# A retention stage with 64-column states, transposes moved between the matmuls of the projections, and own-block scores in front of the state products

## The reference

```python
def chunk_retention(q, k, v, lg, s0, inclusive):        # chunks of 128 tokens
    scores = jnp.einsum('bhnid,bhnjd->bhnij', qc, kc) * dmat[None, :, None]
    o_inner = jnp.einsum('bhnij,bhnje->bhnie', scores, vc)
    wk = jnp.exp((c - 1 - i)[None, :] * lg[:, None])
    u = jnp.einsum('bhnjd,hj,bhnje->bhnde', kc, wk, vc)  # 64 x 64 for each head and chunk
    def step(s, u_n):
        return g_chunk * s + u_n, s
    _, s_prev = lax.scan(step, s0, jnp.moveaxis(u, 2, 0))
    wq = jnp.exp((i + 1)[None, :] * lg[:, None])
    o_cross = jnp.einsum('bhnid,hi,bhnde->bhnie', qc, wq, s_prev)
    return (o_inner + o_cross).reshape(b, h, l, dv)
```

## Time and profile before

| | us |
|---|---|
| median of 3 runs (lowest, highest) | 3538.36 (3535.79, 3541.39) |
| the profiled execution | 3541.91 |
| its span | 3540.1 |
| PE busy in the span | 3165.1 (89%) |
| DVE, ACT, POOL busy | 1487.3, 790.2, 1078.6 |
| mean granted TensorE clock | 0.948 |

### The profile page before, as it was taken

One profiled execution on the slowest core, in us unless ns is written; L12 is line 12 of the kernel. 1 busy time (PEld: TensorE's weight loads), 2 busy tenths in 40 slices (PEclk: granted clock), 3 DMA queues, 4 the chain that ended last, 5 costly groups with the idle time before them and its releaser, 6 DMA issues.

```text
span 3540.1 us, 39903 instructions
## 1 busy us (share of the span) xinstructions
PE 3165.1 (89%) x16718; PEld 2552.8 (72%) x16718; DVE 1487.3 (42%) x1661; ACT 790.2 (22%) x983; POOL 1078.6 (30%) x497
## 2 busy tenths in 40 slices
PE   6986998999789599898888999999699999999959
PEld 5866886787478478787556678787478888888737
DVE  2135508514522631743576630323654044144375
ACT  1110215311220111421134420112222111011241
POOL 1222220023122223023323334343134444444323
PEclk8988999999899799999889999999899999999979
DMA  5200011322021001112121111112111111111111
GB/s 222 72 24 1 30 45 40 109 102 91 22 105 36 7 23 44 49 43 101 36 77 36 36 42 48 38 49 95 71 42 47 48 48 47 48 52 48 60 59 71
DMA packets 57216, 200.64 MB, mean 57 GB/s; under 512 B 5632, under 2 KB 7424, under 8 KB 57088
## 3 DMA queue, kind: packets, MB, share of 16 engines
q1 hardware_dynamic: 40224, 135.81, 11.4%
q10 hardware_dynamic: 16864, 62.97, 4.7%
HBM read 180.93 MB, written 17.83 MB: 56 GB/s over the span
## 4 chain that ended last, share of the span: by engine, by line
issue 40%; PE 34%; POOL 14%; DVE 8%; DMA 2%; ACT 1%; POOLq 0%; ACTq 0%; SPq 0%; DVEq 0%
PE ps L512 26%; POOL w_hi L445 8%; POOL w_lo L447 6%; DVE Sb L1471 3%; PE ps L742 2%; DVE ST L1413 2%; DMA raw<-s 1%; PE ps L659 1%; DMA modfirst<-modw 1%; PE ps L539 1%; PE ps L591 1%; DVE h_lo L1292 1%; DVE kw L1383 1%; PE ps L829 1%; PE ps L763 1%
## 5 line engine op out<-in xcount | busy, mean ns | idle before, releaser
L445 POOL TENSOR_TENSOR w_hi<-raw,pool_zero 128x1024 fp32r<-128x1024 f32 (+1 forms) x228 | 423.5, 1858 | 2260.6 <-PE ps L512 2238.7
L447 POOL TENSOR_TENSOR w_lo<-raw,w_hi 128x1024 fp32r<-128x1024 f32 (+1 forms) x228 | 619.8, 2718 | 17.9
L512 PE MATMUL ps<-g_hi,w_hi 128*128 128x512 f32 x1600 | 503.5, 396 | 37.8 <-DVE g_lo L1292 36.1
L512 PE MATMUL ps<-h_hi,w_hi 128*128 128x512 f32 (+1 forms) x1856 | 474.6, 362 | 56.8 <-DVE h_lo L1292 48.8
L512 PE MATMUL ps<-g_lo,w_hi 128*128 128x512 f32 x1600 | 495.9, 391 | 0.0
L512 PE MATMUL ps<-g_hi,w_lo 128*128 128x512 f32 x1600 | 495.3, 391 | 0.0
L512 PE MATMUL ps<-h_lo,w_hi 128*128 128x512 f32 (+1 forms) x1856 | 455.6, 352 | 0.0
L512 PE MATMUL ps<-h_hi,w_lo 128*128 128x512 f32 (+1 forms) x1856 | 455.2, 352 | 0.0
L512 PEld LDWEIGHTS ps<-h_hi,w_hi 128*128 128x128 f32 x1856 | 305.0, 190 | 128.4 <-issue 63.6
L512 PEld LDWEIGHTS ps<-g_hi,w_hi 128*128 128x128 f32 x1600 | 302.2, 190 | 111.8 <-issue 39.1
L512 PEld LDWEIGHTS ps<-g_lo,w_hi 128*128 128x128 f32 x1600 | 302.8, 189 | 63.6
(11 more groups left out here) (276 smaller groups left out, 3359.8 us busy)
## 6 DMA issues: line engine op xcount, KB each, us to landing
raw<-s SPq DMA_DIRECT2D x212, 512.0 KB, 3.2
modring<-modw ACTq DMA_DIRECT2D x32, 512.0 KB, 4.9
xin<-xT ACTq DMA_DIRECT2D x1, 5120.0 KB, 15.1
x_saved<-Y ACTq DMA_DIRECT2D x1, 5120.0 KB, 17.0
xin<-x_saved ACTq DMA_DIRECT2D x1, 5120.0 KB, 17.8
modfirst<-modw SPq DMA_DIRECT2D x4, 1024.0 KB, 10.9
modfirst<-modw ACTq DMA_DIRECT2D x4, 1024.0 KB, 19.3
x_saved<-Y ACTq DMA_DIRECT2D x1, 4096.0 KB, 11.7
```

What stands on the lines that cost most here:

```text
L445: G.tensor_tensor(w_hi[s][:, :n], raw[s][:, :n], zero.to_broadcast([P, n]), ALU.add).then_inc(hi_done, 1)
L447: G.tensor_tensor(w_lo[s][:, :n], raw[s][:, :n], w_hi[s][:, :n].bitcast(F32), ALU.subtract)\
L512: last = T.matmul(ps[:, o + c0:o + c0 + size], wt[s][:, kk], xx[:, k, t0:t0 + size], start=(k == 0 and n == 0), stop=(k == k_n - 1 and n = ...
```

## The change

Five things, in both layers.
1. **States of 64 columns.** `ST` is 128 x 64 per state: head 0 on partitions 0 to 63, head 1 on 64 to 127. A state product becomes two matmuls of 64 x 64, one per head. A step of the chain becomes one instruction on 128 partitions for both heads, and the two directions alternate, so it waits for the products of both. An output takes one matmul per head and direction with 64 rows and 64 columns of weights, in place of one per direction. The clearing of `ST` goes.
2. **Work moved between the matmuls of slabs.** The rotations move from behind slab g0+6+c to behind k = 7, 6, 5, 4, 3, 2 of it. The values are transposed in three groups of ten tiles inside slabs g0+9 (k = 2 and 5) and g0+11 (k = 2) into banks 0 to 2, and the keys of pair 0 inside slab g0+11 (k = 6). The values of the neighbourhood branch are transposed inside slab g0+18 (k = 2, 4, 6) into banks 3 to 5.
3. **Tables earlier.** DVE's table work stands ahead of the ropes, ACT's behind slab g0+7. Memory is laid out anew for that (`Dm`, `WQ`, `dtmp` in the place of `kw`, `kw` in that of the cosines and sines).
4. **Banks and waits.** Scores and later keys use banks 4 and 5, outputs banks 6 and 7, products banks 0 to 3. The wait for ACT's last copy moves from ahead of slab g0+12 to the first norm matmul in it. POOL's second group of queries no longer waits for the products.
5. **Key weighting** is one tensor_tensor per direction over both heads in place of two tensor_scalar.

```diff
-        ST = at("ST", W_YNA, [P, 2, NT, P])
+        ST = at("ST", W_YNA, [P, 2, NT, HD])
...
-                        if i == 1:
-                            pool.wait_ge(u_ready, 2 * (3 * l + p) + 2)
-                        elif q + i:
+                        if i != 1 and q + i:
                             pool.wait_ge(o_ready, q + (1 if i else 0))
...
+                for c in range(6):
+                    def beside(k):
+                        if l == 0 and c == 0 and k == 4:
+                            turn_modulation(1, [7 * BANK, 7 * BANK + P])
+                        if k == (7, 6, 5, 4, 3, 2)[c]:
+                            if l == 0 and c == 0:
+                                pe.wait_ge(mod_added, 1)
+                            rotate(c)
+                        if c == 3 and k in (2, 5):
+                            if k == 2:
+                                pe.wait_ge(evac_done, g0 + 9)
+                            turn_values(6 * l + k // 3, 0)
+                        if c == 5 and k == 2:
+                            pe.wait_ge(evac_done, g0 + 11)
+                            turn_values(6 * l + 2, 0)
+                        if c == 5 and k == 6:
+                            pe.wait_ge(vt_used, 6 * l + 3)
+                            for gi in range(3):
+                                turn_pair_keys(0, gi)
+                    if c == 4:
+                        pe.wait_ge(vt_used, 6 * l + 2)
+                    slab(g0 + 6 + c, c % 2, h_hi, h_lo, KD, (FULL, part)[c % 2], 3, between=beside)
+                pe.wait_ge(evac_done, g0 + 12)
...
                         for x, d in enumerate(terms):
-                            T.matmul(ps[:, c:c + P], ST[:, d, STATE_AT[d](n), :], qw[i % 2][:, d, t * P:(t + 1) * P],
-                                     start=(t == 0 and x == 0), stop=False, skip_group_check=True)
+                            for a in range(2):
+                                r = slice(HD * a, HD * (a + 1))
+                                T.matmul(ps[r, c:c + P], ST[r, d, STATE_AT[d](n), :], qw[i % 2][r, d, t * P:(t + 1) * P],
+                                         start=(t == 0 and x == 0), stop=False, skip_group_check=True)
...
                         for x, n in enumerate(BACK if d else range(NT - 1)):
-                            b = 3 * d * BANK + x * P
-                            last = T.matmul(ps[:, b:b + P], kw[:, d, n, :], Vt[:, n, p * P:(p + 1) * P],
-                                            start=True, stop=True)
+                            for a in range(2):
+                                c = 2 * d * BANK + x * HD
+                                last = T.matmul(ps[HD * a:HD * (a + 1), c:c + HD], kw[:, d, n, HD * a:HD * (a + 1)],
+                                                Vt[:, n, p * P + HD * a:p * P + HD * (a + 1)], start=True, stop=True,
+                                                skip_group_check=True)
                         last.then_inc(u_ready, 1)
...
-                pe.wait_ge(o_used, o_groups(l, PAIRS))
...
+                slab(g0 + G_NA + 6, 0, h_hi, h_lo, KD, part, 3, between=values)
+                pe.wait_ge(vt_used, 6 * l + 6)
...
+                    dve.wait_ge(u_ready, 2 * (3 * l + p) + 2)
+                    for x in range(NT - 1):
+                        for d in range(2):
+                            c = 2 * d * BANK + x * HD
+                            if x == 0:
+                                ins = V.tensor_copy(ST[:, d, 0, :], ps[:, c:c + HD])
+                            else:
+                                ins = V.scalar_tensor_tensor(ST[:, d, x, :], ST[:, d, x - 1, :], gch[:, 3 * d + p:3 * d + p + 1],
+                                                             ps[:, c:c + HD], ALU.mult, ALU.add)
```

More of the change, by code:

```diff
@@ L576, in _ @@
                         slab(j * 2 + (g0 + s), s, h_hi, h_lo, KD, (FULL, part)[s], 3, between=gates if l == 0 else None)
[L577 to L592, removed]
-                                            start=True, stop=True)
-                        last.then_inc(rot_ready, 1)
@@ L596, in _ @@
[L596 to L610, removed]
@@ L612, in _, with turn_values @@
-                transpose_values(18 * l)
-                pe.wait_ge(vt_used, 18 * l + 9)
-                ku = 9 * l
+                def turn_values(unit, base):
+                    if unit % 3:
+                        pe.wait_ge(vt_used, unit)
+                    for n in range(NT):
+                        last = T.transpose(ps[:, base * BANK + n * P:base * BANK + (n + 1) * P],
+                                           VT[:, unit % 3, n * P:(n + 1) * P], ident)
+                    last.then_inc(vt_ready, 1)
@@ L616, in turn_pair_keys, with rotate @@
+                def rotate(c):
+                    pe.wait_ge(tab_in, 48 * (l + 1))
+                    pe.wait_ge(rope_done, 6 * l + c + 1)
+                    for half in range(2):
+                        last = T.matmul(ps[:, (6 + half) * BANK:(7 + half) * BANK], ret_const[:, 0, :],
+                                        QK[:, c, CTX + 512 * half:CTX + 512 * (half + 1)], start=True, stop=True)
+                    last.then_inc(rot_ready, 1)
                 def turn_pair_keys(p, gi):
@@ L618, in turn_pair_keys @@
                     n0, cnt = GROUPS[gi]
[L619 to L624, removed]
+                    u = 9 * l + 3 * p + gi
+                    if p == 0:
+                        bank = gi
+                    else:
+                        bank = 4 + (3 * p + gi) % 2
+                        if 3 * p + gi >= 5:
+                            pe.wait_ge(kt_used, u - 1)
+                        if gi == 0:
+                            pe.wait_ge(sd_ready, o_groups(l, p))
@@ L714, in _, with values @@
                         slab(j * 2 + (g0 + G_NA + s), s, h_hi, h_lo, KD, FULL, 3, between=norms)
-                slab(g0 + G_NA + 6, 0, h_hi, h_lo, KD, part, 3)
-                pe.wait_ge(evac_done, g0 + G_NA + 6)
-                transpose_values(18 * l + 9)
+                def values(k):
+                    if k == 2:
+                        pe.wait_ge(evac_done, g0 + G_NA + 6)
+                    if k in (2, 4, 6):
+                        turn_values(6 * l + 3 + (k - 2) // 2, 3)
+                slab(g0 + G_NA + 6, 0, h_hi, h_lo, KD, part, 3, between=values)
+                pe.wait_ge(vt_used, 6 * l + 6)
                 slab(g0 + G_NA + 7, 1, h_hi, h_lo, KD, part, 3)
@@ L1006, in _ @@
-                evac_values(18 * l)
+                    if c == 1:
+                        evac_values(6 * l, 0)
+                        evac_values(6 * l + 1, 0)
+                    if c == 2:
+                        evac_values(6 * l + 2, 0)
+                    evac_part(g0 + 7 + 2 * c, Y[:, 2 + c, :], ACT.Silu)
+                    if c == 0:
+                        act.wait_ge(dtab, l + 1)
+                        lgl = lg[:, 18 * l:18 * l + 18]
+                        A.activation(Dm[:], dtmp[:], ACT.Exp)
+                        for d in range(2):
+                            for p in range(PAIRS):
+                                x = 12 + 3 * d + p
+                                A.activation(WQ[:, d, p, :], ret_const[:, 3 + d, :], ACT.Exp, scale=lgl[:, x:x + 1])
+                        own.link(A.activation(wk[:], wk[:], ACT.Exp))
+                        A.activation(gch[:], lgl[:, 12:18], ACT.Exp, scale=float(P)).then_inc(wtab, 1)
@@ L1038, in _ @@
                     taken(1, VT)
+                for c in range(3):
+                    evac_values(6 * l + 3 + c, 3)
                 act.wait_ge(bias_clear, 2 * l + 1)
```

129 lines of the change are left out of this document (54 added, 75 removed).

## The result

| | before | changed |
|---|---|---|
| median, us (lowest to highest, runs) | 3539.3 (3535.79 to 3541.39, 4) | 3449.28 (3448.16 to 3450.42, 4) |
| profiled execution | 3541.91 | 3448.83 |
| span | 3540.1 | 3445.9 |
| PE busy in the span | 3165.1 (89%) | 3131.7 (91%) |
| mean granted TensorE clock | 0.948 | 0.957 |

The ratio is 0.9747, with a 95% interval of 0.973 to 0.9764: 90 us faster, where 61 were forecast.

A forecast was written before the change was run, and what follows sets the result against it. The retention stage was taken as bound by a chain across engines for which PE waits. Savings of 30.2 us in layer 0 and 30.8 in layer 1, together 61.0, took the median 3538.36 to 3477, given as 3478; range 3463 to 3500.

The forecast's parts named there:

- the copy of slab 11: Behind slab 11 PE first waits for ACT's copy of it: 1.5 us in layer 0, 1.3 in layer 1.
- the weighting: Key weighting of the first pair: four tensor_tensor of 512 columns and two of half the size, 3.4 us in all.
- POOL hidden: POOL's weight split and queries behind slab 11 finish before they are needed, with 6 us spare.
- slab 12 right behind the last outputs: At the stage's end PE no longer waits for ACT's last copy: 1.1 us saved in each layer.
- Products 4.36 to the chain's start: In each retention pair, the chain starts 4.36 us after the products, since it waits for both directions.
- no change, nearest to the 64-column row: The 72 recorded loads of narrow products take 3.9 us, the same as the 4.09 before.
- the lower bound of 2.0 us: Products of a pair if only the moving columns counted, now half: 2.0 us, 2.1 less.
- rival 2: Products at half their time and a warm clock during the chain's wait: 3458 to 3470, chance 0.16.
- That is one half, 5.53: The chain of states, nine steps of two instructions for both directions together, takes 5.53 us per pair.
- 0.197 each: Price of a transpose moved into a slab; 40 of them make 7.9 us, in slabs lengthened by 10.2 per layer.
- The values of the neighbourhood branch: Their 30 transposes, moved into the slab, cost 6.0 + 0.3 us: 0.4 and 0.7 lost, perhaps 0.1 for the last copy.
- Rivals 1, 3 and 4: Narrow tiles no faster, 3502 or 3525, chance 0.12; clock falls inside slabs, 3614, 0.02; moved work meets waits in slabs, 3498, 0.06.

The follow-up runs named there:

- e2: Changed kernel with all nine state products of one head ahead of those of the other, within each direction: 3454.1 us.
- e4: Changed kernel with each chain instruction on 128 partitions split by head into two on 64, direction outer, head inner: 3489.1 us.
- e3: Changed kernel with the products of both directions of a step in neighbouring columns of one PSUM bank: 3449.01 us.
- e6: Changed kernel with each chain instruction split by head into two on 64 partitions, head outer, direction inner: 3474.06 us.
- e5: Changed kernel with all chain steps of one direction, then the other, the first starting when its own products are done: 3448.62 us.
- e1: Changed kernel with each value transpose issued twice in a row, 120 more in all, inside slabs: 3464.22 us.
- v6: Changed kernel with the matmuls of the second scores issued four times, in the time in which PE idles: 3432.93 us.
- v9: Changed kernel with v8's order and waits, and the second scores issued twice in layer 0 and three times in layer 1: 3428.03 us.
- v1: Changed kernel with products issued step by step, both directions together, and the chain starting behind the first four steps: 3437.32 us.
- v8: Changed kernel with products step by step as in v1, the chain starting once its first step's products are done: 3432.08 us.
- e7: Changed kernel with rotations back behind their slabs and the first pair's values and keys transposed behind slab 11, narrow states kept: 3485.33 us.

## Why the prediction was wrong

What was right: the stage as a row of waits, the copy of slab 11 as the first wait (1.3 to 1.5), the weighting (3.15 for six against 3.4), POOL hidden, slab 12 right behind the last outputs, the clock full in the slabs, and the direction. The steps that failed are three prices in the sum, all off in one direction.

1. **"Products 4.36 to the chain's start."** It was 2.36 (239.75 to 242.11), 2.0 less in each of six pairs, 12 us. I took "no change, nearest to the 64-column row" and left the lower bound of 2.0 us as rival 2. The price holds for two products of the same head: e2 shows 0.052 per record where I gave 0.054. That it is the loads that set this pace was argued, and no run tests it. But products of two heads write different halves of the partitions and run together. The Trainium skill, TensorE: Matmul & The Clock Gate, "What overlaps and what doesn't", has it that a weight load overlaps a running matmul only in other row groups. The trace disagrees: the 72 loads, all on the same 128 rows, take 2.18 us, and their matmuls 2.32 in the same stretch (rows at 239.74 and 259.29; the end of a matmul is modelled in the profile).
2. **"That is one half, 5.53."** It was 4.42, 1.1 less per pair, 6.6 us. Halving the instructions was right. What the halving left out is that the old chain's neighbours changed the half of the partitions at every instruction and so started 0.302 and 0.322 apart (e4), while two directions on the same partitions start 0.20 apart (e3 on 128, e6 on 64). My bounds for it, "the same" and 0.7 more, left nothing below the half. In e5 the forecast's 5.53 comes out, as 5.43, because there each instruction waits for the last.
3. **"0.197 each" for transposes.** That mean had the waits for ACT in it: PE was idle in 1.6 of the 5.90 us for 30. In a slab nothing waits, and e1 gives 0.11 to 0.12. The slabs got 6.1 longer in each layer and not 10.2: 4.1 x 2 = 8.2. The values of the neighbourhood branch won 2.6 and 2.3 where 0.4 and 0.8 were to be lost: 6.1.

Together 12 + 6.6 + 8.2 + 6.1 = 32.9; with the 61 of the forecast 94, and the spans differ by 94.2. That it closes so well is in part luck: the profiled execution before lay 2.6 above its median, the medians differ by 90, and parts that the change does not touch move by some us between profiles.

Rival 2 was nearest, by its first half. Its second half, a clock that stays full since PE idles less, did not come: the clock still fell in every pair, and only in the second of layer 0 after the first outputs. v6 and v9 show that this was there to be had, 1.8 us a pair in v6. There PE idled 0.75 to 1.65 us before the first outputs and the clock never fell in the two stages; in v1, with 2.27 and 2.49, it fell in none of three pairs and in all three; in v8, with 1.94 and 2.17, in two and in all three; in the changed kernel, with 3.4 to 3.7, in all six. What else decides beside the idle time is open. Rivals 1, 3 and 4 fell: no row of the slabs runs below the full clock or waits.

## What to carry to other kernels

Look for the rate of an instruction in its distance to the next start, not in its length, and ask for each neighbour whether it uses the same partitions and whether it depends on the one before. A price for work that is to be moved is to be taken from a row without waits. Where PE waits for a chain on another engine, count what it costs twice: the wait, and the slower matmuls behind it; either can be worked on by itself, as v6 did with the second and v8 with the first. Whether the clock falls is to be read from the trace, not from the length of the wait alone.

## What the runs showed of the hardware

- Products of 64 columns in pairs that go to different halves of the partitions: 72 records in 2.18 us, 7 and 52 ns apart (changed kernel). The same without the alternation: 3.74 us, 58 ns apart (e2).
- On DVE, 128 or 64 partitions and 64 columns, an operation of 0.27 to 0.29 us: 0.20 from start to start if independent and on the same partitions (e3, e6), 0.30 to 0.32 if independent and on the other half (e4, e6), 0.317 if dependent (e5). Two PSUM banks or one made no difference (e3).
- 126 matmuls that do nothing new made the kernel 16.6 us faster (v6). 10.8 us of it lie in the two stages whose granted clock went from 0.88 and 0.90 to 1.00; the rest is not explained.
- The same ten transposes took 1.25 us at a granted clock of 1.00 and 2.40 at 0.50 (e7).
